# A decoder layer in fp32 on one core: the feed-forward up and down products by seven products of half blocks instead of eight

## The reference

```python
def hybrid_mixer(x, w_in, ...):            # conv group + mLSTM group, then w_out
    ...
def conv_ffn(x, w_up, w_ffn_conv, b_ffn_conv, w_down):
    hid = jnp.einsum('bsd,df->bsf', x, w_up)            # 2048 -> 2 x 5632
    hid = causal_dwconv(hid, w_ffn_conv, b_ffn_conv)    # width 3 over positions
    val, gate = hid[..., :D_FF], hid[..., D_FF:]
    return jnp.einsum('bsf,fd->bsd', jax.nn.silu(gate) * val, w_down)   # 5632 -> 2048
...
mix = hybrid_mixer(x, ...)
x = layer_norm(alpha * x + mix, ln1_g, ln1_b)
ff = conv_ffn(x, ...)
x = layer_norm(alpha * x + ff, ln2_g, ln2_b)
```

## Time and profile before

| | |
|---|---|
| median of 3 runs | 2343.01 us |
| the profiled execution, first to last instruction | 2341.3 us, 1.7 below the median |
| mean granted TensorE clock | 0.994 of full |
| TensorE busy | 2302.4 us (98%), 10248 matmuls |
| weight loads busy | 1895.4 us (81%) |
| VectorE busy | 1099.8 us (47%) |
| ScalarE busy | 588.2 us (25%) |
| GpSimd busy | 103.9 us (4%) |
| DMA | 249.55 MB, mean 107 GB/s |

### The profile page before, as it was taken

One profiled execution on the slowest core, in us unless ns is written; L12 is line 12 of the kernel. 1 busy time (PEld: TensorE's weight loads), 2 busy tenths in 40 slices (PEclk: granted clock), 3 DMA queues, 4 the chain that ended last, 5 costly groups with the idle time before them and its releaser, 6 DMA issues.

```text
span 2341.3 us, 24919 instructions
## 1 busy us (share of the span) xinstructions
PE 2302.4 (98%) x10248; PEld 1895.4 (81%) x10248; DVE 1099.8 (47%) x1130; ACT 588.2 (25%) x488; POOL 103.9 (4%) x62
## 2 busy tenths in 40 slices
PE   8999999999999998999999999999999999999996
PEld 7888888888888887888888888888888888888885
DVE  4354324433345569544444444544444444444448
ACT  4323222221133352222221212222221212222221
POOL 0000000000000039000000000000000000000003
PEclk9999999999999999999999999999999999999998
DMA  5322222232336532222222222222222222222231
GB/s 222 108 90 73 92 98 79 90 127 90 107 137 223 193 149 73 107 99 98 90 101 96 90 102 95 90 94 103 90 95 102 90 97 100 90 90 107 90 126 72
DMA packets 37151, 249.55 MB, mean 107 GB/s; under 512 B 4092, under 2 KB 4124, under 8 KB 7920
## 3 DMA queue, kind: packets, MB, share of 16 engines
q1 hardware_dynamic: 35984, 242.24, 28.9%
q0 software_dynamic: 1120, 6.64, 0.8%
HBM read 244.67 MB, written 4.19 MB: 106 GB/s over the span
## 4 chain that ended last, share of the span: by engine, by line
PE 95%; DVE 3%; DMA 1%; ACT 0%; issue 0%; POOL 0%; SPq 0%; DVEq 0%; ACTq 0%
PE ps L948 32%; PE ps L949 32%; PE ps L950 31%; DVE w_lo L567 1%; DMA raw<-w_mix 1%; DVE stream L886 0%; DVE stream L883 0%; PE ps L1148 0%; ACT w_hi L382 0%; DVE x_full L866 0%; DVE stream L816 0%; PE ps L1006 0%; POOL act_lo L354 0%; PE ps L978 0%; PE ps L977 0%
## 5 line engine op out<-in xcount | busy, mean ns | idle before, releaser
L948 PE MATMUL ps<-act_hi,w_hi 128*128 128x512 f32 (+1 forms) x2080 | 806.5, 388 | 10.0 <-DVE w_lo L567 6.2
L382 ACT ACTIVATE w_hi<-raw 128x2048 fp32r<-128x2048 f32 x220 | 421.8, 1917 | 1527.2 <-PE ps L950 1524.6
L949 PE MATMUL ps<-act_lo,w_hi 128*128 128x512 f32 (+1 forms) x2080 | 804.1, 387 | 0.0
L950 PE MATMUL ps<-act_hi,w_lo 128*128 128x512 f32 (+1 forms) x2080 | 804.0, 387 | 0.0
L567 DVE TENSOR_TENSOR w_lo<-raw,w_hi 128x2048 fp32r<-128x2048 f32 x219 | 512.9, 2342 | 358.3 <-ACT w_hi L382 358.3
L948 PEld LDWEIGHTS ps<-act_hi,w_hi 128*128 128x128 f32 x2080 | 392.1, 189 | 92.3 <-DVE w_lo L567 6.8
L950 PEld LDWEIGHTS ps<-act_hi,w_lo 128*128 128x128 f32 x2080 | 391.9, 188 | 79.1
L949 PEld LDWEIGHTS ps<-act_lo,w_hi 128*128 128x128 f32 x2080 | 392.1, 188 | 78.3
L949 PE MATMUL ps<-w_lo,h_hi 128*128 128x512 f32 x704 | 280.9, 399 | 0.0
L948 PE MATMUL ps<-w_hi,h_hi 128*128 128x512 f32 x704 | 277.4, 394 | 0.0
L950 PE MATMUL ps<-w_hi,h_lo 128*128 128x512 f32 x704 | 275.9, 392 | 0.0
(11 more groups left out here) (142 smaller groups left out, 1018.8 us busy)
## 6 DMA issues: line engine op xcount, KB each, us to landing
raw<-w_up SPq DMA_DIRECT2D x88, 1024.0 KB, 4.7
raw<-w_mix SPq DMA_DIRECT2D x56, 1024.0 KB, 4.7
raw<-w_down SPq DMA_DIRECT2D x44, 1024.0 KB, 4.7
raw<-w_out SPq DMA_DIRECT2D x32, 1024.0 KB, 4.7
stream<-x_rows POOLq DMA_DIRECT2D x2, 2048.0 KB, 10.4
stream<-x_t SPq DMA_DIRECT2D x3, 1024.0 KB, 13.7
ln_rows<-ln_rows POOLq DMA_DIRECT2D x2, 1024.0 KB, 7.0
ln_rows<-ln_rows SPq DMA_DIRECT2D x2, 1024.0 KB, 7.8
```

Of the source, the lines that this page charges most:

```text
L382: act.activation(w_hi[:, s % SPLIT, :], raw[:, s % RAW, :], ACT.Copy).then_inc(tile_hi, 1)
L948: pe.matmul(dst, a[0], b[0], start=first, stop=False)
L949: pe.matmul(dst, a[0], b[1], start=False, stop=False)
L950: return pe.matmul(dst, a[1], b[0], start=False, stop=last)
```

## The change

**The idea.** For a 2 x 2 grid of blocks, a product needs eight block products; by Strassen's method seven are enough, if sums of blocks are multiplied and their results added up in the right places. Here (Winograd's form) the seven are `P1` to `P7`, with four sums of weight blocks and four of activation blocks.

**Up.** A group is a pair of tiles (value and gate features of one hidden tile): its weights are the four blocks A11, A12 (value, first and second half of the 2048 inputs), A21, A22 (gate), 128 x 1024 each. The other factor is the first norm's output in four blocks (half of the inputs x 256 positions), whose four sums are made once and kept split (`xb`, 7 blocks). Per group the seven products are 8 x 3 matmuls each, of 256 columns. A result that belongs in two places is accumulated further in PSUM or added by ScalarE and VectorE to the hidden tile in `hid`. Three slots hold the split block in use and the next ones (`AHEAD` = 2). The taps of the convolution now read `hid` in SBUF.

**Who makes the weight sums.** Per group A21 + A22, A11 - A21 and the first minus A11 on GpSimd; A12 minus the third on VectorE (`last_combination`).

**Down.** The hidden tiles are stored to memory, and read back as blocks; the 44 of them are worked in six chunks of `CHUNK_PAIRS` pairs. Per pair seven slots, a slot is 12 matmuls of 512 columns. All four weight sums and the four sums of hidden blocks are on GpSimd (in the first chunk the first weight sum is VectorE's, `first_s1`). VectorE adds 1024 columns at a time from PSUM to `acc` (`add_out`). Five slots, split four ahead.

**Around it.** The residual moves out of the window: the normed rows are stored to memory, and in eight pieces of 128 x 1024, one in every second up group, read, scaled and shifted on GpSimd, and stored again; `acc` starts from them. All loops over groups are written out.

```diff
-FCH = 4
-GROUPS = D_FF // P // FCH
+NF = D_FF // P
+GROUPS = NF - 1
+ORDER = ("P1", "P2", "P6", "P5", "P7", "P3", "P4")
+AHEAD = 2
+CHUNK_PAIRS = [4, 4, 4, 4, 4, 2]
+DOWN_SLOTS, DOWN_AHEAD = 5, 4
...
 # SyncE
+            for m in range(1, GROUPS - 1):
+                store_hidden(m - 1)
+                load_unit(m + 2)
+                if m >= 3 and m % 2 and (m - 3) // 2 < PIECES:
+                    load_residual((m - 3) // 2)
+                if m >= 4 and m % 2 == 0 and (m - 4) // 2 < PIECES:
+                    store_residual((m - 4) // 2)
...
 # GpSimd
+            for m in range(1, GROUPS + 1):
+                u = unit[m % 2]
+                pool.wait_ge(gate_in[m % 2], 16 * (loads_before(m) + 1))
+                pool.tensor_tensor(u[:, AX, :], u[:, A21, :], u[:, A22, :], ALU.add).then_inc(s1_up, 1)
+                pool.wait_ge(s1_up, m)
+                pool.wait_ge(val_in[m % 2], 16 * (loads_before(m) + 1))
+                pool.tensor_tensor(u[:, A21, :], u[:, A11, :], u[:, A21, :], ALU.subtract).then_inc(s3_up, 1)
+                pool.wait_ge(s3_up, m)
+                pool.wait_ge(up_lo, NP * (m - 1) + 1)
+                pool.tensor_tensor(u[:, A11, :], u[:, AX, :], u[:, A11, :], ALU.subtract).then_inc(s2_up, 1)
...
 # ScalarE
+            def up_split(n):
+                m, i = unit_of(n)
+                if n >= 3:
+                    act.wait_ge(up_done, n - 2)
...
+                act.activation(slot_hi[(n + 2) % 3][:, :], unit[m % 2][:, BLOCK[ORDER[i]], :], ACT.Copy).then_inc(up_hi, 1)
...
+            for n in range(N_UP):
+                m, i = unit_of(n)
+                if n and ORDER[(n - 1) % NP] in ("P1", "P6", "P5", "P4"):
+                    hid_copy(n - 1)
+                if n + AHEAD < N_UP:
+                    up_split(n + AHEAD)
+                if m > 1 and i < 2:
+                    first_tap(m - 1, i)
+                if m > 1 and i == 3:
+                    silu(m - 1)
...
 # VectorE
+            for n in range(N_UP):
+                m, i = unit_of(n)
+                if n and ORDER[(n - 1) % NP] in ("P2", "P7", "P3"):
+                    hid_add(n - 1)
+                if n + AHEAD < N_UP:
+                    up_lo_part(n + AHEAD)
+                if ORDER[i] == "P2":
+                    last_combination(m)
...
+                if m > 1 and i in (1, 2):
+                    later_taps(m - 1, i - 1)
+                if m > 1 and i == 4:
+                    gated(m - 1)
...
 # TensorE, up and down
+                for j in range(8):
+                    last = mm3(ps[:, up_bank(m, i), 0:256], (hi[:, P * j:P * j + P], lo[:, P * j:P * j + P]),
+                               (xb[:, i, 0, j, :], xb[:, i, 1, j, :]), fresh and j == 0, j == 7, not fresh)
+                last.then_inc(up_done, 1)
...
+                for q in range(2):
+                    last = mm3(ps[:, (0 if k % 2 else 4) + 2 * u + q, :],
+                               (h[:, 0, p, P * u:P * u + P], h[:, 1, p, P * u:P * u + P]),
+                               (hi[:, 512 * q:512 * q + 512], lo[:, 512 * q:512 * q + 512]), fresh, p == g - 1,
+                               what not in ("P1", "P2", "P5"))
```

More of the change, by code:

```diff
@@ L63 @@
 FF0 = N_MIX + N_OUT
-GR0 = FF0 + 2
 CONV0 = MIX.index(("conv", 0, 0))
@@ new lines, in _ @@
+            hid_split(0, 0)
+            down_split(0)
+            hid_copy(N_UP - 1)
+            first_tap(GROUPS, 0)
+            first_tap(GROUPS, 1)
+            for s in range(1, DOWN_AHEAD):
+                down_split(s)
+                if s == 1:
+                    silu(GROUPS)
+            for s in range(N_DOWN):
+                c, i, p = DOWN[s]
+                if p == 0:
+                    k = NP * c + i + 1
+                    if k < NP * CHUNKS:
+                        hid_split(k // NP, k % NP)
+                if s + DOWN_AHEAD < N_DOWN:
+                    down_split(s + DOWN_AHEAD)
@@ new lines, in down_product @@
+            def down_product(s):
+                c, i, p = DOWN[s]
+                what, g, k = ORDER[i], CHUNK_PAIRS[c], NP * c + i
+                pe.wait_ge(down_lo, s + 1)
+                if p == 0:
+                    pe.wait_ge(hc_lo, k + 1)
+                    if k == 0:
+                        pe.wait_ge(hid_dve, 3 * GROUPS)
+                    elif k == 1:
+                        pe.wait_ge(hid_act, 4 * GROUPS)
+                    else:
+                        pe.wait_ge(added, 2 * (k - 1))
+                for u in range(2):
+                    last = down_half(s, u)
+                last.then_inc(down_done, 1)
@@ new lines, in _ @@
+            for n in range(N_UP):
+                up_product(n)
+            end = N_DOWN - CHUNK_PAIRS[CHUNKS - 1]
+            for s in range(end):
+                down_product(s)
+            k = NP * CHUNKS - 1
+            pe.wait_ge(hc_lo, k + 1)
+            pe.wait_ge(added, 2 * (k - 1))
+            for u in range(2):
+                for s in range(end, N_DOWN):
+                    if u == 0:
+                        pe.wait_ge(down_lo, s + 1)
+                    last = down_half(s, u)
+                last.then_inc(half_done, 1)
```

839 lines of the change are left out of this document (595 added, 244 removed).

## The result

The changed kernel takes 2499.66 us (median of 4 runs, 2498.28 to 2503.3) against 2343.06 (2342.16 to 2343.12) for the kernel before on the same chip: ratio 1.0672, 95% interval 1.0657 to 1.0687. Forecast were 2452 and +109; measured were +157. The profiled execution is the longest of the four; it spans 2501.5 us, 1.8 less than its own time.

What follows compares the result with a forecast made beforehand. TensorE bounds the kernel before; after the change, turns between VectorE and GpSimd cost time. 2341.3 + 80 (up) + 20 (into up) + 14 (up to down) - 8 (down) + 3 (end) = 2450.3, plus 1.7: 2452 us; range 2290 to 2545.

Steps and rivals of the forecast that it cites:

- They take turns: VectorE operations with two SBUF inputs and GpSimd operations never run together; 1024 columns cost 1.14 and some 2.25 us.
- A group is 22.8 us: Up stage: 20.16 us of TensorE plus a 2.6 us stall before P7's product; bounds 20.16 and 23.5.
- I take 35: Up stage: the residual's extra GpSimd work and its delays add 35 us, bounds 5 and 45.
- P6's product can start near 917: Into the up stage: VectorE's queue and GpSimd's sums delay this product from 889, a net +20 us (12 to 30).
- -8: Down stage: VectorE bounds chunks at 88.5 us, 485 us in all, 8 us saved (-26 to +13).
- +14: Passage from up to down: the fourth slot's low part comes at 24.2 us, due 8.4; 14 us lost (8 to 25).
- +3: End of the kernel: GpSimd's tail waits for the last output rows' statistics and VectorE's queue; 3 us (0 to 6).
- the turns fit: Rival, 28%: GpSimd's sums fall in VectorE's idle time; groups 20.16 to 21, chunks 78.4 to 84.9, total 2243 to 2327.
- The clock falls in every stall: Rival, 7%: half clock after each stall costs 2 to 3 us a group, total 2538 to 2581.
- 188 ns loads: Rival, 2%: long rows of 256-column products go at the weight loads' pace, 31.6 us a group, total about 2790.
- over 85%: Sign for the forecast: VectorE busy more than this share of the up stage, low parts averaging well over 1.2 us.
- a half clock in steady groups: Sign that the forecast is wrong: TensorE at half clock in the up stage's steady groups.

Runs made afterwards that it cites:

- e1: The changed kernel with weight sums (up groups from the third, down chunks) and hidden-block sums moved from GpSimd to VectorE; GpSimd keeps the residual: 2326.59 us.
- e3: The changed kernel without GpSimd's three weight sums in up groups from the third on (that part of the result is not computed): 2375.39 us.
- e4: The changed kernel with each GpSimd weight sum in up groups from the second on replaced by two constant fills that read nothing: 2370.76 us.
- e6: The changed kernel with 12 more 256-column matmuls before TensorE's wait for P7's low part in groups 3 to 42: 2486.11 us.
- e2: The changed kernel with those sums and the residual's product and sum on VectorE, the residual's scaling on ScalarE: 2286.89 us.

## Why the prediction was right, point by point

Direction, main cause and range were right: it was the likeliest case. The size was 51 us short (2501.5 in the profiled execution against the sum 2450.3). By stages: the way into up -5, the rest of up +23 (1032 us from the start of the first group's P6 product to the first down matmul, against 1009), down with the passage to it +28 (526.7 us against 485 + 14), the end +7; they add up to 53, 2 more than the miss. By its steps:

- **"They take turns"** (VectorE and GpSimd exclude each other): right, shown by e1, e3 and e4. Prices of 1.14 and 2.25 hold (3.42 = 2.28 + 1.14). The price of an add of 1024 columns from PSUM was put at 1.25; the slope it names gives 1.22, and 1.21 was measured.
- **"A group is 22.8 us", a stall before P7's product:** 23.18. The stall is there and ended by `slot_lo`, 0.8 to 2.8 us long. It goes with the landing of the weights as worked out: where GpSimd's pair starts 3.5 us into the group it is 1.6 (predicted 1.6 at 3), where 5.7, 2.6 (predicted 2.6 at 5.5). But the start swings between 1.6 and 5.8, and the mean stall is 2.0. The half clock, left out of the sum, takes 0.8: that 22.8 came so close is in part two errors that offset each other, though with the clock held up (e6) a group took 22.94, less than 0.2 from the forecast. 23 groups: 9 us more than forecast.
- **"I take 35" for the residual:** the term that was off most in up, 16 groups 416 us instead of 400. Each piece's two operations of GpSimd hold VectorE in its unbroken stretch: groups with a piece take 28.3, those between 23.7. Even with the weight sums gone it costs 39.7 (e2).
- **Into up, "P6's product can start near 917":** 912.1, 5 us better, with `t1raw` at 4.49 us instead of 2.28, the turns again.
- **"-8" for down:** about 17 us short. The three middle chunks take 92.3 us each instead of 88.5, the fifth 86.0, and the last, half as long, 52.3 instead of 44.3. The step that failed: GpSimd, at work 0.8 of the time, hides 14 of 17.6 us of adds. It is at work for 0.69 (63.6 of 92): it waits 28 us a chunk for low parts, adds in those gaps hide nothing, and only 10.4 of 16.9 us of adds lie beside a sum. That is some 3 of the 3.8 us. The adds themselves run beside GpSimd as assumed (1.21 us each). In the last chunk VectorE also takes the statistics of the output rows (8.2 us), which stand in no term.
- **Up to down, "+14":** the fourth slot's low part was done 23.6 us after the first slot, predicted 24.2, and TensorE had waited 14.9; but nothing was given back, 6.8 us more of waits follow. About +21; the whole first chunk took 111.4 us, 13.5 more than 88.5 - 4.6 + 14.
- **The end, "+3":** from the start of TensorE's last matmul to the end 30.7 us instead of 20.8: +10. VectorE's backlog at 2471 and the turns of `finish` with GpSimd's tail were priced too small.
- **Rival "the turns fit":** it did not come, as GpSimd's pair starts 1.6 to 5.8 us into a group, and the rival needs it behind 9.9. In e1, where VectorE makes the sums, steady groups do take 20.16, but that is another change. **"The clock falls in every stall":** it falls behind the stall in 11 of the 23 steady groups, and fillers before P7 gave back 11 to 14 us (e6). **"188 ns loads":** wrong, in 750 us of e2 loads are busy for 749.84 and matmuls start every 0.120.
- **The signs:** two did not come out. VectorE was busy for 82% of the up stage, not over 85%. And "a half clock in steady groups", named as a sign of being wrong, was there in those 11 groups.

Not run: the change with GpSimd's pair begun later in a group, which is the condition of the first rival; fillers in the down stage, so what that stage's mean clock of 0.94 costs is open; and the up-to-down passage by itself.
